# The weighted sums of three modulation tiles: from one fused instruction on VectorE to a product and a sum on GpSimd

## The reference, cut to what matters

```python
def hybrid_layer(x, c, ..., w_ada, b_ada, ...):
    mod = jax.nn.silu(c) @ w_ada + b_ada            # [1, 3072], w_ada is [1024, 3072]
    shift, scale, gate = jnp.split(mod[:, None, :], 3, axis=-1)
    h = rms_norm_2(x, norm_g) * (1 + scale) + shift
    ...
    return x + gate * y
```

## Time and profile before

| | |
|---|---|
| time, median of 3 runs | 1912.29 us (1894.81, 1912.29, 1915.6) |
| span of the profiled execution, first to last instruction | 1900.3 us |
| mean granted TensorE clock | 0.976 of full speed |
| busy: TensorE, VectorE, ScalarE, GpSimd | 1792.4, 1512.8, 1151.9, 59.4 us |
| stage with the modulation sums | 223 to 412 us of the span |

### The profile page before, as it was taken

How to read it: one execution, slowest core, us unless ns; L and a number is a source line. 1 busy time by engine, 2 the same in 40 slices (tenths; PEclk the granted TensorE clock), 3 DMA queues, 4 the chain that set the end, 5 groups by cost and what they waited for, 6 DMA issues and landing times.

```text
span 1900.3 us, 26823 instructions
## 1 busy us (share of the span) xinstructions
PE 1792.4 (94%) x10110; PEld 1506.5 (79%) x10110; DVE 1512.8 (80%) x1440; ACT 1151.9 (61%) x1105; POOL 59.4 (3%) x84
## 2 busy tenths in 40 slices
PE   7987899999978999999999999999999998988988
PEld 7976777878766888888888888888888887776777
DVE  6885678886757888888897888988898886786685
ACT  5661543444656676767677676767677664565554
POOL 2000011101100000000000000000000000000000
PEclk9996999998988999999999999999999999999999
DMA  6405579974216999999999999899999993522531
GB/s 229 133 3 101 177 272 328 339 253 145 92 67 228 380 341 359 379 345 361 370 335 373 346 360 378 329 376 340 362 368 353 359 355 107 180 70 81 165 107 45
DMA packets 162270, 488.80 MB, mean 257 GB/s; under 512 B 8506, under 2 KB 13755, under 8 KB 162192
## 3 DMA queue, kind: packets, MB, share of 16 engines
q1 hardware_dynamic: 153536, 457.91, 66.4%
q0 software_dynamic: 8656, 29.82, 4.8%
HBM read 485.07 MB, written 2.62 MB: 257 GB/s over the span
## 4 chain that ended last, share of the span: by engine, by line
PE 67%; DVE 13%; issue 10%; ACT 5%; DMA 4%; POOL 0%; DVEq 0%; ACTq 0%; POOLq 0%
PE bank L1166 20%; PE bank L1168 20%; PE bank L1167 20%; DVE weights_at L1966 4%; DMA BIG<-in_e_ffn_up 2%; ACT weights_at L2954 2%; DVE BIG L2346 2%; DMA BIG<-in_e_ffn_down 2%; PE bank L1696 2%; PE bank L1761 1%; PE bank L1378 1%; ACT BIG L3173 1%; DVE x_low L1993 1%; ACT YT L2931 0%; DVE BIG L2386 0%
## 5 line engine op out<-in xcount | busy, mean ns | idle before, releaser
L2600 DVE TENSOR_TENSOR expert_weights_low<-BIG,expert_weights_high 128x2048 fp32r<-128x2048 f32 x336 | 750.8, 2287 | 57.4 <-ACT expert_weights_high L3249 57.0
L3249 ACT ACTIVATE expert_weights_high<-BIG 128x2048 fp32r<-128x2048 f32 x336 | 625.8, 1922 | 75.7 <-DMA BIG<-in_o_moe_up 41.3
L1166 PE MATMUL bank<-expert_weights_high,expert_x_high 128*128 128x512 f32 x896 | 352.0, 393 | 3.0 <-DVE expert_x_low L2665 2.9
L1168 PE MATMUL bank<-expert_weights_low,expert_x_high 128*128 128x512 f32 x896 | 349.5, 390 | 0.0
L1167 PE MATMUL bank<-expert_weights_high,expert_x_low 128*128 128x512 f32 x896 | 349.4, 390 | 0.0
L2954 ACT ACTIVATE weights_at<-BIG 128x2048 fp32r<-128x2048 f32 (+2 forms) x100 | 183.5, 1835 | 176.3 <-DMA BIG<-in_e_ffn_down 38.0
L1966 DVE TENSOR_TENSOR weights_at<-BIG,weights_at 128x2048 fp32r<-128x2048 f32 (+2 forms) x100 | 219.1, 2191 | 84.4 <-ACT weights_at L2954 82.4
L1166 PE MATMUL bank<-weights_at,x_high 128*128 128x512 f32 (+2 forms) x608 | 243.1, 400 | 20.0 <-DVE x_low L1993 7.0
L1168 PE MATMUL bank<-weights_at,x_high 128*128 128x512 f32 (+2 forms) x608 | 238.5, 392 | 0.0
L1167 PE MATMUL bank<-weights_at,x_low 128*128 128x512 f32 (+2 forms) x608 | 238.3, 392 | 0.0
L1166 PEld LDWEIGHTS bank<-expert_weights_high,expert_x_high 128*128 128x128 f32 x896 | 168.4, 188 | 37.2 <-DVE expert_x_low L2665 3.1
(11 more groups left out here) (412 smaller groups left out, 2113.4 us busy)
## 6 DMA issues: line engine op xcount, KB each, us to landing
BIG<-in_o_moe_gate SPq DMA_DIRECT2D x112, 1024.0 KB, 5.2
BIG<-in_o_moe_up SPq DMA_DIRECT2D x112, 1024.0 KB, 5.8
BIG<-in_o_moe_down SPq DMA_DIRECT2D x112, 1024.0 KB, 5.6
BIG<-in_w_ada POOLq DMA_DIRECT2D x48, 512.0 KB, 4.9
BIG<-in_w_in SPq DMA_DIRECT2D x20, 1024.0 KB, 5.0
BIG<-in_o_w_qkv SPq DMA_DIRECT2D x12, 1024.0 KB, 5.1
BIG<-in_e_w_in SPq DMA_DIRECT2D x10, 1024.0 KB, 5.0
BIG<-in_e_ffn_gate SPq DMA_DIRECT2D x10, 1024.0 KB, 5.0
```

Of the source, the lines that this page charges most:

```text
L1166: mm(b, high_l, high_r, start=start, stop=False, skip_group_check=not check)
L1168: last = mm(b, high_l, low_r, start=False, stop=stop, skip_group_check=not check)
L2600: tt_(E_WL[q % E_SLOTS], half(q % E_SLOTS), E_WH[q % E_SLOTS].bitcast(F32), SUB).then_inc(w_low, 1)
L3249: f(E_WH[q % E_SLOTS], half(q % E_SLOTS), ACT.Copy).then_inc(w_high, 1)
```

## The change

GpSimd makes the sums itself, in the loop that also loads the pieces. The fused instruction becomes two, a product of the piece with the scalar, in place in its slot, and an addition into `ADAS[i]`; each is followed by a wait for its own completion. `ada` and all its calls are gone from VectorE. `inverse_root(2)` now stands behind the 22nd piece and in front of the last two; the four `diff_root` and all that follows them stand behind all 24. The number and order of the DMAs is the same.

```diff
+        ada_scaled = sem("ada_piece_scaled")
...
-            def modulation_weights(first, end):
-                for q in range(first, end):
-                    i, k = divmod(q, KD)
-                    if q >= ADA_SLOTS:
-                        pool.wait_ge(ada_used, q - ADA_SLOTS + 1)
-                    for h in range(2):
...
+            def modulation_weights(q):
+                i, k = divmod(q, KD)
+                for h in range(2):
...
+            def modulation_sum(q):
+                i, k = divmod(q, KD)
+                piece = ADAW[q % ADA_SLOTS]
+                pool.wait_ge(ada_loaded[q % ADA_SLOTS], 32 * (q // ADA_SLOTS + 1))
+                if k == 0:
+                    g.tensor_scalar(ADAS[i], piece, s_cc[:, 0:1], None, ALU.mult).then_inc(ada_used, 1)
+                else:
+                    g.tensor_scalar(piece, piece, s_cc[:, k:k + 1], None, ALU.mult).then_inc(ada_scaled, 1)
+                    pool.wait_ge(ada_scaled, q - i)
+                    g.tensor_tensor(out=ADAS[i], in0=ADAS[i], in1=piece, op=ALU.add).then_inc(ada_used, 1)
+                pool.wait_ge(ada_used, q + 1)
 
             pool.wait_ge(filled, PLAN.filled(("Up", 0, 1)))
-            modulation_weights(0, ADA * KD)
-            inverse_root(2)
+            for q in range(ADA_SLOTS):
+                modulation_weights(q)
+            pool.wait_ge(c_silu, 1)
+            for q in range(ADA * KD):
+                modulation_sum(q)
+                if q + ADA_SLOTS < ADA * KD:
+                    modulation_weights(q + ADA_SLOTS)
+                if q == ADA * KD - 3:
+                    inverse_root(2)
             for hf in range(2):
                 diff_root(hf, 0)
                 diff_root(hf, 1)
...
-            ada_done = [0]
-            def ada(n):
-                for q in range(ada_done[0], ada_done[0] + n):
-                    i, k = divmod(q, KD)
-                    w_ = ADAW[q % ADA_SLOTS]
-                    v.wait_ge(ada_loaded[q % ADA_SLOTS], 32 * (q // ADA_SLOTS + 1))
-                    if k == 0:
-                        v.wait_ge(c_silu, 1)
-                        V(ts(ADAS[i], w_, s_cc[:, 0:1], None, MUL), ada_used)
-                    else:
-                        V(stt(ADAS[i], w_, s_cc[:, k:k + 1], ADAS[i], MUL, ADD), ada_used)
-                    ada_done[0] = q + 1
...
                 if c == last_c - 1:
                     modulation(0)
-                if c:
-                    ada(1)
                 low()
-                if c:
-                    ada(1)
...
                     low()
-                    ada(1)
                     down(c - 1, 1)
                     low()
-                    ada(1 if c == 1 else 2)
             down(last_c, 0)
```

More of the change, by code:

```diff
@@ L1101, in _ @@
             inverse_root(1)
-            def modulation_weights(first, end):
-                for q in range(first, end):
-                    i, k = divmod(q, KD)
-                    if q >= ADA_SLOTS:
-                        pool.wait_ge(ada_used, q - ADA_SLOTS + 1)
-                    for h in range(2):
[L1110 to L1113, removed]
-            pool.wait_ge(filled, PLAN.filled(("Up", 0, 1)))
-            modulation_weights(0, ADA * KD)
-            inverse_root(2)
+            def modulation_weights(q):
+                i, k = divmod(q, KD)
+                for h in range(2):
+                    l, n0 = divmod(i * ADA_W + h * 1024, 3 * D)
+                    src = I["w_ada_2"][l][k * P:(k + 1) * P, n0:n0 + 1024]
+                    pool.dma_start(ADAW[q % ADA_SLOTS][:, h * 1024:(h + 1) * 1024], src)\
+                        .then_inc(ada_loaded[q % ADA_SLOTS], 16)
+            def modulation_sum(q):
[9 more added lines that the diff above has]
+                pool.wait_ge(ada_used, q + 1)
+            pool.wait_ge(filled, PLAN.filled(("Up", 0, 1)))
+            for q in range(ADA_SLOTS):
[7 more added lines that the diff above has]
+                    inverse_root(2)
             for hf in range(2):
```

## The result

The median is 1961.6 us over four runs (1955.3 to 1972.9), against 1908.0 us over four runs of the kernel before (1894.8 to 1915.6). The recorded ratio, which weighs all runs, is 1.029, with a 95% interval of 1.025 to 1.033 (of the two medians it is 1.028): 53.6 us slower. The forecast was 1926 us and its range ended at 1957.

A forecast was written before the change was run, and what follows sets the result against it. TensorE bounds the kernel, the weight chain (load, high, low) just fast enough behind it. GpSimd's 219 us from 230 put the root at 449, 14 us lost: 1912.3 + 14 = 1926 us, range 1900 to 1957.

The forecast's parts named there:

- When GpSimd reaches the root: At `inverse_root(2)` behind 22 pieces: 219 us of GpSimd work from 230, root at 449 us, some 20 us late.
- 22 issues and waits: On GpSimd, each piece costs 1.05 us of load issuing and 0.5 us of waiting, 34 us for 22 pieces.
- the price of the product: GpSimd's product of 128x2048 floats takes 2.1 us, bounds 1.98 to 3.96; 46 us for 22.
- The charge of 55 us: From 230 to 429 us VectorE's lows keep GpSimd out for 55 us, bounds 0 and 73.6.
- The addition: GpSimd's addition of 128x2048 floats takes 4.4 us, bounds 1.98 to 5.9; 84 us for 19.
- TensorE's 5.8 us in hand: At the fourth qkv tile: its low ended at 434.5, TensorE wanted the tile at 440.3 us.
- Small losses from lows held up: In the feed-forward stage, small losses from lows held by additions are swallowed by the wait for the late root.
- the lows are the new bound: Rival: some 30 lows each wait 2 us for an addition, TensorE loses up to 30 us; 1925 to 1942, chance 0.08.
- the 14: At the fourth qkv tile: root at 449, low ends at 454.2, 14 us behind TensorE's need; the whole forecast loss.
- dearer instructions: Rival: product 3.0 us, addition 5.0, root at 480, time 1957; at the upper bounds 1995; chance 0.28.
- `modulation(1)`: On TensorE at 395.7 us: GpSimd's sixteen pieces are done at 396, so no wait but no room either.
- GpSimd in time: Rival: lows don't hold GpSimd, 22 pieces end at 394 us, TensorE wins 3.8 us; 1908, chance 0.22.

The follow-up runs named there:

- writes-only run: Changed kernel with every GpSimd product replaced by three memsets and every addition by two, sums not made: 1936.4 us, ratio 1.018.
- the additions alone: Changed kernel without its 21 products on GpSimd, pieces added unscaled (3 products and 21 additions stay): 1936.8 us, ratio 1.018.
- the run with the clock at 0.50: Changed kernel with GpSimd's product made by the two-input instruction, the scalar broadcast along the row: 1954.0 us, ratio 1.027.
- the run with additions as writes: Changed kernel without the 21 products, each addition made two memsets and each first product of a tile three: 1904.8 us, ratio 1.002.
- the piece loads unpaced: Changed kernel with 21 products and 21 additions left out, loads and the first product of each tile kept: 1919.6 us, ratio 1.006.

## Why the prediction was wrong

The direction of the forecast's mechanism was right; its size was off, by two terms of "When GpSimd reaches the root" and by a rival that was true at the same time.

**The terms of the sum.** The forecast had the root at 449, it began at 484.1:

| term | forecast | measured |
|---|---|---|
| start of the first product | 230 | 231.6 |
| 22 products | 22 x 2.1 = 46 | 22 x 5.45 = 120 |
| 19 additions | 19 x 4.4 = 84 | 19 x 4.49 = 85 |
| 22 issues and waits | 22 x 1.55 = 34 | 22 x 1.55 = 34 (the undisturbed period, 461.15 to 472.64, is 11.49; less 5.45 and 4.49) |
| held by VectorE | 55 | 484.1 - 231.6 - 239 = 13 |

- **The step that failed is the price of the product**, 2.1 us "since the memset is the nearest row": it is 74 us too low in all, and 5.45 lies outside the stated bounds of 1.98 to 3.96. A memset of the same size took 1.81 us here, so the write says nothing of an instruction that also reads and computes. The sum took the lower end where the two ends were a factor of two apart.
- **The charge of 55 us** for VectorE's lows is 42 us too high. It read the short roots rightly (they wait for VectorE) but took it for both. With long instructions on GpSimd's side mostly GpSimd is in work when a low comes, and it is the low that waits. "Whether VectorE waits in the same way for GpSimd the trace can't say" was the open question, and the answer is the other half of the result. The two errors offset each other by more than half.
- **The addition**, 4.4 against 4.49, is right. The Trainium skill's 4497 ns (GPSIMD Engine Reference, "Elementwise — side-by-side cycle accounting") agrees with the trace to 0.01 us.
- **TensorE's 5.8 us in hand** are borne out by the writes-only run: a root 32.6 us behind its input, a gap of 26.4. In the changed kernel nothing is left of them: TensorE stops 7.2 us behind the mean squares, not 11 (they are themselves held for 4.1 us), and the first low ends 8.3 us behind the root, so the gap is 25.6 at a root 24.4 us late. With the measured root the forecast's own step gives 484.1 - 435.1 = 49 us, 1961 us. That this is the measured median is in part luck, for the sum leaves out what stands next.

**What the sum left out.** "Small losses from lows held up" weren't small. The rival "the lows are the new bound" said up to 30 us and only beyond the 14; the additions alone cost 31 by the medians, 24 of them seen up to the next root. It had 0.08, since 53 us of VectorE's time were freed and VectorE waited 34 us for ScalarE. Both are true and beside the point: slack of an engine is no help when each instruction of its chain must find a gap, and the chain load, high, low, load is in series. In the whole change most of it is hidden: the mean squares, 30 us late, still come 24 us before the root.

**The clock.** The forecast let TensorE resume at once. Behind the gap the granted clock is lower (0.76 over the 40 us behind the root, in which TensorE is busy for 27.8; before, the 40 us behind its root had 0.91, with 39.0 us busy). From this root to the next one it took 149.4 us before, 157.7 with the change and 164.4 in the run with the clock at 0.50. In those 8.4 us are the clock and the last two pieces, whose instructions hold lows and gains (first low of the fourth tile 8.3 us behind the root instead of 5.2); no run separates them. The remainder between the two profiled spans, 70.7 - 54.8 - 8.4 = 7.5 us, lies behind that, 5.8 of them in the last stretch (from 1809.5 us on) with the same work as before at a granted clock of 0.90 instead of 0.98, in a run of after that was the slowest of its four.

**The other steps.** The rival "dearer instructions" was the nearest: it decided from 0.12 us an instruction and had 1957 at a product of 3.0; the product alone passed its upper bound, but the hold it kept at 55 made up for it. `modulation(1)` waited 1.2 us, as forecast no room and no real wait. "GpSimd in time" is out. Its gain of 3.8 us isn't seen either: the run with additions as writes, which had everything in its favour, is at best 1 us faster by its interval. The range missed by 5 us because its upper end used the middle prices (1957), while the text itself had worked out 1995 at the upper bounds.

## What to carry to other kernels

- Work moved from VectorE to GpSimd isn't priced by GpSimd's idle time. Ask first how long one of its reading instructions lasts against the period of VectorE's two-input instructions on the critical chain; if the first is close to the second, each of them may pass only once in a gap, and the stage then takes GpSimd's period, as it did here.
- An unseen price with bounds a factor of two apart, multiplied by 22, is a range of 40 us; take the range from both ends. And an idle engine's list with a small, urgent instruction at its end (a root of two numbers) makes the whole list urgent.

## What the runs showed of the hardware

- A product of 128x2048 floats with one scalar for each partition takes GpSimd 5.45 us, longer than the sum of two such tiles (4.49), or than the same product written with two inputs (4.05 mean). A memset of that size takes 1.81, a sum of 128x512 1.33 with VectorE idle and 1.98 beside lows.
- The exclusion between a low and a reading instruction of GpSimd is not even. A low that comes during an addition ends some 2.15 us behind its end, during a product 0.4 us behind it (let in some 1.9 us early); the low pays 1.6 us on the mean and GpSimd 0.3 to 0.4 (1.3 an addition where the product has two inputs too). Even VectorE's instructions of 2 to 16 elements wait: 0.16 us became 4.27, and eight of them 16.6 instead of 1.64.
- Loads issued sooner aren't free: with the piece loads unpaced the DMA share went from 0.90 to 0.97, weight loads took 7.4 to 10.7 us instead of 5.9 to 6.6, and the mean squares came 18.6 us later. How much of that run's 14 us this is, no run shows.
